# Both weight buffers start 64 bytes further within each partition

## The chip, the cores and the metric

The kernel runs on one core of one Trainium2 chip. The metric is the device time of one execution in microseconds (us); below is the median of three executions. The five engines of the core are called TensorE (PE in the profile, with PEld for its weight loads), VectorE (DVE), ScalarE (ACT), GpSimd (POOL) and SyncE (SP, which issues nearly all the loads here).

## The reference

Two transformer blocks run one after the other on a sequence of 256 tokens of width 1024, all in float32. Cut to what matters:

```
x = x + 0.5 * swiglu(rmsnorm(x), w_gate, w_up, w_down)          # "ff1", d_ff 2816
proj = rmsnorm(x) @ w_in                                        # q, k, v, gMLP and gate inputs
x = x + (g_a * (gmlp(proj) @ w_branch_a) + g_b * (stick(q, k, v) @ w_branch_b)) @ w_out
x = x + 0.5 * swiglu(rmsnorm(x), ...)                           # "ff2"
x = rmsnorm(x)
h = x + moba(rmsnorm(x) @ w_qkv) @ w_o[0]                       # "moba"
h = h + relu(rmsnorm(h) @ w_up[0]) ** 2 @ w_down[0]             # "mlp0", d_ff 4096
h = h + fox(rmsnorm(h) @ w_q, rmsnorm'(h) @ w_kv) @ w_o[1]      # "fox": q and k, v from two norms
h = h + relu(rmsnorm(h) @ w_up[1]) ** 2 @ w_down[1]             # "mlp1"
out = rmsnorm(h)
```

Nearly all the arithmetic is in products of 256 token rows with weight matrices, some 217 MB of weights that are each read once.

## The kernel before

**The weight stream.** Every weight matrix comes in units of at most 128 partitions x 1024 float32. SyncE loads a unit into one of six slots of the tile raw. ScalarE copies it, rounded to the shorter format float32r, into one of eight slots of w_hi (the helper `hi`, line 595). VectorE subtracts, so that w_lo holds the rest (the helper `lo`, line 936). TensorE then takes three products for one: high weights times high activations, high times low and low times high. The semaphores hi_ready, lo_ready and used pass a slot from one to the next, always in the same order of units, which is written out by hand for each engine.

**Which operand is which.** A matmul has a stationary operand, loaded ahead of it into the array by a weight load (LDWEIGHTS, 128 columns), and a moving one, that streams through (256 or 512 columns here). There are three uses of the weights:

- In the first products of the four feed-forward stages (the function `up`), weights are stationary and the transposed activations xt move. Line 1500 takes w_hi times xt_hi and xt_lo together, 512 columns; line 1507 takes w_lo times xt_hi, 256 columns. One chunk has four units, and a unit has eight matmuls of line 1500 and then eight of line 1507 (the fourth unit of a chunk takes them in twos). There are 11 chunks in ff1 and ff2 each and 8 in mlp0 and mlp1 each, 38 in all.
- In the projections of q and k (the function `project`, the shared line 1414), weights are stationary, 128 x 128 at a time, and xt moves with 256 columns, in 24 matmuls a unit. In fox, q is not computed from xt but from xq_hi and xq_lo, and k from xt. A cycle of the attention loop has one unit for q and one for k, 48 matmuls back to back. Three attention stages have 8 such pairs of units each.
- Everywhere else (the functions `rows_times`, `down` and `out_unit`, also line 1414), the activations (xt, yt_hi, yt_lo, ht_hi, ht_lo) are stationary, and weights move, 512 columns.

**Where the tiles lie.** Each tile is a run of bytes in every partition, and tiles lie one behind another in the order of the code, each start rounded up to 32 bytes. Before the change raw, w_hi, w_lo, x, side, xt, yt_hi, yt_lo, ht_hi, ht_lo, the three work tiles, qt, kt, vn and the constants all start at a multiple of 128 bytes, and every slice that a matmul takes of them starts at a multiple of 128 bytes too. Small tiles behind them break this order. So these start 64 bytes past a multiple of 128: xq_hi, xq_lo, dist and nslope, and in the first block a_uv, gates and wst, which share their place. wf_hi and wf_lo (16 columns a slice, line 1414 too) start at a multiple of 128.

Of the kernel before, what the change touches and what calls it, by code (L numbers as in the profile page):

```python
# [25 lines left out]
P = 128  # L26
# [116 lines left out]
def two_blocks(nc, x_in, ff1_norm, ff1_w_gate, ff1_w_up, ff1_w_down, mix_norm, w_in, b_gate, gmlp_ln_g,  # L143
# [4 lines left out]
    with ctx:  # L148
        def sb(name, shape, dt=F32, scope=ctx):
            return scope.enter_context(nc.sbuf_tensor(name, shape, dt))  # L150
# [3 lines left out]


        raw = sb("raw", [P, RAW, WIDE])
        w_hi = sb("w_hi", [P, RING, WIDE], F32R)
        w_lo = sb("w_lo", [P, RING, WIDE], F32R)
        x = sb("x", [P, TOK, D])
        side = sb("side", [P, TOK, D])  # L160
        xt = sb("xt", [P, KT, 2, S], F32R)
# [1757 lines left out]
```

How the kernel before makes its waits and increments, by code:

```python
        def consumed(eng, c, i=0):  # L274
            eng.wait_ge(s["used"], RING + c + 1 + RING * i)
# [4 lines left out]
        @block.sync  # L281
# [1 line left out]
            def room(c, i):  # L283
                sp.wait_ge(s["lo_ready"], RING + c - RAW + 1 + RING * i)
# [80 lines left out]
            def norm_rows():  # L366
                sp.wait_ge(s["sp_done"], HEADS)
                sp.wait_ge(s["r_ready"], HEADS)
                for row, dst in zip((gmlp_ln_g, gmlp_ln_b), ln_rows):
                    sp.dma_start(dst, row.rearrange("a g c -> a (g c)").broadcast_to([P, D])).then_inc(s["blk1_in"], 16)
# [58 lines left out]
            proj_units("w_out", wout, lambda i: 0)  # L430
            ff_units("ff2", ff2_w_gate, ff2_w_up, ff2_w_down)
            att_units("moba", *qkv_moba)
            out_units("w_o0", wo[0])
            mlp_units("mlp0", w_up_2[0], w_down_2[0])
            att_units("fox", *qkv_fox)
            out_units("w_o1", wo[1])
            mlp_units("mlp1", w_up_2[1], w_down_2[1])
            for tok in range(TOK):
                sp.wait_ge(s["second_out"], tok + 1)
                sp.dma_start(out[0, tok * P:(tok + 1) * P, 512:D], side[:, tok, 512:D]).then_inc(s["stored"], 16)
            sp.wait_ge(s["stored"], 32 * TOK)
# [6 lines left out]
            def const(ins, name="const_done"):  # L449
                ins.then_inc(s[name], 1)
                count["n"] += 1
                pool.wait_ge(s[name], count["n"])
# [79 lines left out]
            def pairs(phase):  # L533
                if phase == "fox":
                    pool.wait_ge(s["cn_done"], 1)
                if phase != "stick":
```

## Time and profile before

| | |
|---|---|
| median of 3 executions | 1236.98 us (1236.93 to 1237.11) |
| the profiled execution's own time | 1236.78 us |
| its span, first to last instruction | 1235.0 us |
| TensorE matmul busy | 1222.5 us, 6847 matmuls |
| TensorE weight load busy | 1048.1 us |
| VectorE busy | 835.0 us |
| ScalarE busy | 627.7 us |
| mean DMA rate | 180 GB/s |
| granted TensorE clock | 1.000 of full |

The busy time of TensorE counts each matmul from its start to a modelled end, and these overlap: a matmul of 512 columns is shown with 389 ns while the next one starts some 227 ns after it. So "busy" says that TensorE always has something under way, not that it runs at its peak. What sets the pace within a run of matmuls is the distance from one start to the next.

### The profile page before, as it was taken

Reading aid. Unit: us, or ns where it says so; the run is one execution under the profiler, and the core shown is the slowest. Engines: PE = TensorE matmul, PEld = TensorE weight load, DVE = VectorE, ACT = ScalarE, POOL = GpSimd, SP = SyncE. Lnnn points to the kernel's source line nnn. Section 1 sums busy time; section 2 is a strip of 40 time slices with the busy share of each in tenths; the row PEclk is TensorE's granted clock in tenths of the full one; section 3 lists DMA queues with packets and bytes.
Section 4 is the critical chain, followed back from the end, with each engine's and each line's share of the span. In section 5 each row is a group of like instructions: output and inputs, shape, how many; then the busy total and the mean of one; then the engine's idle time right before and its main releaser. Section 6 shows DMA issues by size and latency. Waiting matters only on the chain.

```text
span 1235.0 us, 17596 instructions
## 1 busy us (share of the span) xinstructions
PE 1222.5 (99%) x6847; PEld 1048.1 (85%) x6847; DVE 835.0 (68%) x1277; ACT 627.7 (51%) x965; POOL 82.9 (7%) x181
## 2 busy tenths in 40 slices
PE   8999999999999999999999999999999999999998
PEld 7888888898888888888888988888888888888886
DVE  6877766454675668777775766875656676876764
ACT  6544446565553446444455656544446455744443
POOL 0000000121000000000003210000000540000000
PEclk9999999999999999999999999999999999999999
DMA  7755666534855555655665445866653655676640
GB/s 237 238 184 186 204 193 194 183 115 115 294 173 169 170 155 175 214 179 186 194 195 169 123 136 188 261 195 191 189 171 105 173 155 166 198 246 189 191 148 35
DMA packets 174923, 221.74 MB, mean 180 GB/s; under 512 B 9100, under 2 KB 103912, under 8 KB 174840
## 3 DMA queue, kind: packets, MB, share of 16 engines
q1 hardware_dynamic: 173496, 216.86, 56.0%
q0 software_dynamic: 912, 2.71, 0.8%
q8 instruction: 54, 0.88, 0.3%
q10 hardware_dynamic: 432, 1.05, 0.2%
q14 instruction: 29, 0.24, 0.1%
HBM read 219.52 MB, written 1.06 MB: 179 GB/s over the span
## 4 chain that ended last, share of the span: by engine, by line
PE 95%; DVE 3%; ACT 1%; DMA 0%; issue 0%; ACTq 0%; DVEq 0%; POOLq 0%
PE bank L1414 55%; PE bank L1500 22%; PE bank L1507 11%; PE bank L1437 1%; PE bank L1671 1%; DVE w_lo L936 1%; PE bank L1654 1%; DVE xt L971 1%; PE bank L1644 1%; PE bank L1631 1%; PE bank L1629 1%; DVE x L1051 0%; PE bank L1675 0%; ACT xt L633 0%; DMA gain_rows<-in_ff_norm 0%; PE bank L1622 0%
## 5 line engine op out<-in xcount | busy, mean ns | idle before, releaser
L936 DVE TENSOR_TENSOR w_lo<-raw,w_hi 128x1024 fp32r<-128x1024 f32 (+1 forms) x448 | 491.4, 1119 | 199.8 <-ACT w_hi L595 199.5
L595 ACT ACTIVATE w_hi<-raw 128x1024 fp32r<-128x1024 f32 (+1 forms) x448 | 422.6, 972 | 277.9 <-PE bank L1507 141.7
L1500 PE MATMUL bank<-xt,w_hi 128*128 128x512 f32 x1216 | 317.0, 393 | 0.0
L1500 PEld LDWEIGHTS bank<-xt,w_hi 128*128 128x128 f32 x1216 | 216.3, 189 | 34.6
L1507 PEld LDWEIGHTS bank<-xt,w_lo 128*128 128x128 f32 x1216 | 170.6, 190 | 15.3
L1507 PE MATMUL bank<-xt,w_lo 128*128 128x256 f32 x1216 | 175.1, 282 | 0.0
L1414 PE MATMUL bank<-w_hi,xt 128*128 128x512 f32 x512 | 159.8, 393 | 0.9 <-DVE xq_lo L971 0.5
L1414 PE MATMUL bank<-w_hi,yt_lo 128*128 128x512 f32 x336 | 132.2, 394 | 0.0
L1414 PE MATMUL bank<-w_hi,yt_hi 128*128 128x512 f32 x336 | 130.9, 390 | 0.0
L1414 PE MATMUL bank<-w_lo,yt_hi 128*128 128x512 f32 x336 | 130.9, 390 | 0.0
L1414 PE MATMUL bank<-xt,w_hi 128*128 128x256 f32 x640 | 116.0, 283 | 0.0
L1414 PEld LDWEIGHTS bank<-w_hi,xt 128*128 128x128 f32 x512 | 94.6, 188 | 23.1 <-issue 3.7
L1414 PE MATMUL bank<-w_lo,xt 128*128 128x512 f32 x256 | 99.8, 390 | 0.0
L1414 PEld LDWEIGHTS bank<-xt,w_hi 128*128 128x128 f32 x640 | 99.5, 191 | 0.2
L989 DVE TENSOR_REDUCE work<-bank 128x256 f32<-128x512 f32 x152 | 96.1, 683 | 0.0
L1414 PE MATMUL bank<-xt,w_lo 128*128 128x256 f32 x320 | 91.8, 287 | 0.0
L1414 PE MATMUL bank<-w_hi,ht_lo 128*128 128x512 f32 x224 | 87.3, 390 | 0.0
L1414 PE MATMUL bank<-w_hi,ht_hi 128*128 128x512 f32 x224 | 87.3, 390 | 0.0
L1414 PE MATMUL bank<-w_lo,ht_hi 128*128 128x512 f32 x224 | 87.2, 389 | 0.0
L1414 PEld LDWEIGHTS bank<-w_hi,yt_lo 128*128 128x128 f32 x336 | 63.1, 188 | 13.9 <-issue 1.0
L1414 PEld LDWEIGHTS bank<-w_lo,yt_hi 128*128 128x128 f32 x336 | 63.1, 188 | 13.3
L1414 PEld LDWEIGHTS bank<-w_hi,yt_hi 128*128 128x128 f32 x336 | 63.1, 188 | 12.9
(197 smaller groups left out, 1149.1 us busy)
## 6 DMA issues: line engine op xcount, KB each, us to landing
raw<-in_w_up SPq DMA_DIRECT2D x64, 512.0 KB, 4.2
raw<-in_w_down SPq DMA_DIRECT2D x64, 512.0 KB, 4.5
raw<-in_w_in SPq DMA_DIRECT2D x56, 512.0 KB, 4.6
raw<-in_ff_w_gate SPq DMA_DIRECT2D x88, 256.0 KB, 3.5
raw<-in_ff_w_up SPq DMA_DIRECT2D x88, 256.0 KB, 4.4
raw<-in_ff_w_down SPq DMA_DIRECT2D x88, 256.0 KB, 4.6
raw<-in_moba_w_qkv SPq DMA_DIRECT2D x24, 512.0 KB, 4.1
raw<-in_w_o SPq DMA_DIRECT2D x16, 512.0 KB, 3.8
```

Of the source, the lines that this page charges most:

```text
L595: act.activation(w_hi[:, c % RING, 0:w], raw[:, c % RAW, 0:w], ACT.Copy).then_inc(s["hi_ready"], 1)
L936: dve.tensor_tensor(w_lo[:, c % RING, 0:w], raw[:, c % RAW, 0:w], w_hi[:, c % RING, 0:w].bitcast(F32), ALU.subtract).then_inc(s["lo_ready" ...
L971: dve.scalar_tensor_tensor(low[:, k, :], src, gain[:, 8 * g + k:8 * g + k + 1], high[:, k, :].bitcast(F32), ALU.mult, ALU.subtract)\
L989: dve.tensor_reduce(work[0][:, q // 2, (q % 2) * S:(q % 2 + 1) * S], up_banks(m)[q][:].rearrange("p (a b) -> p b a", a=2), AX_X, ALU.add)\
L1414: ins = pe.matmul(dst, p, q, start=first and n == 0, stop=last and n == 2)
L1437: ins = pe.transpose(banks[b][:, o:o + P], src[:, tok, k * P:(k + 1) * P], ident[:])
L1500: ins = pe.matmul(up_banks(m)[q][:], w_h[:, k % 2, q * P:(q + 1) * P], flat(xt[:, k, :, :]), start=k == 0, stop=False, skip_group_check=True)
L1507: ins = pe.matmul(up_banks(m)[q][:, 0:S], w_l[:, k % 2, q * P:(q + 1) * P], xt_hi[:, k, :], start=False, stop=k == KT - 1, skip_group_chec ...
L1629: pe.matmul(z[:, 0:P], q[:, 0:P], k[:, 0:P], start=True, stop=True)
L1631: ins = pe.matmul(z[:, P:3 * P], q[:, P:S], k[:, 0:S], start=False, stop=True, skip_group_check=True)
L1644: pe.matmul(z[:, 0:S], ntri[:], sp[:, h, 0:S], start=False, stop=True, skip_group_check=True)
L1654: ins = pe.transpose(t_bank[h][:, o * P:(o + 1) * P], work[1][:, h, o * P:(o + 1) * P], ident[:])
```

## The change

An unused tile of 64 bytes a partition is put between raw and w_hi, and another behind w_lo. w_hi and w_lo start 64 bytes further than before, hence 64 bytes past a multiple of 128. All tiles behind them start 128 bytes further, so their places modulo 128 are what they were. raw stays where it was. No instruction is added, removed or moved, and no order or wait changes.

```diff
         raw = sb("raw", [P, RAW, WIDE])
+        gap_in = sb("gap_in", [P, 16])
         w_hi = sb("w_hi", [P, RING, WIDE], F32R)
         w_lo = sb("w_lo", [P, RING, WIDE], F32R)
+        gap_out = sb("gap_out", [P, 16])
         x = sb("x", [P, TOK, D])
```

For the two operands of a matmul that means: xt, yt and ht lay a multiple of 128 bytes from the weights that they meet, and now lie an odd multiple of 64 bytes from them. xq_hi and xq_lo lay an odd multiple of 64 bytes from them, and now lie a multiple of 128.

## Rows read from the trace of the kernel before

**Rows 1.** The page: span, busy time by engine, chain by engine.
```profile
span 1235.0 us, 17596 instructions
PE 1222.5 (99%) x6847; PEld 1048.1 (85%) x6847; DVE 835.0 (68%) x1277; ACT 627.7 (51%) x965; POOL 82.9 (7%) x181
...
PE 95%; DVE 3%; ACT 1%; DMA 0%; issue 0%; ACTq 0%; DVEq 0%; POOLq 0%
```

**Rows 2.** Waits by engine: who for whom, us in total, times, longest.
```profile
DVE w_lo L936 <- ACT w_hi L595: 199.5, 149, 6.2
ACT w_hi L595 <- PE bank L1507: 141.7, 85, 2.2
...
PE bank L1437 <- DVE x L1051: 1.1, 3, 0.4
...
PE bank L1414 <- DVE xt L971: 0.3, 2, 0.2
```

**Rows 3.** Line 1414 by form: duration min/median/max in ns, first and last start.
```profile
L1414 PE MATMUL bank<-xt,w_hi x640: 274/283/287, 208.6 to 1023.2; 128*128 128x256 f32 x160
...
L1414 PE MATMUL bank<-xt,w_lo x320: 277/283/388, 208.5 to 1022.9; 128*128 128x256 f32 x160
...
L1414 PE MATMUL bank<-w_hi,ht_hi x224: 387/389/395, 35.1 to 1217.6; 128*128 128x512 f32 x112
...
L1414 PE MATMUL bank<-xq_hi,w_hi x64: 276/276/282, 949.8 to 1020.2; 128*128 128x256 f32 x64
L1414 PE MATMUL bank<-xq_lo,w_hi x64: 276/276/281, 949.9 to 1020.3; 128*128 128x256 f32 x64
L1414 PE MATMUL bank<-xt,wf_hi x16: 276/276/279, 947.1 to 949.6; 128*16 128x256 f32 x16
```

**Rows 4.** Lines 1500 and 1507, the same columns.
```profile
L1500 PE MATMUL bank<-xt,w_hi x1216: 387/389/775, 11.0 to 1206.9; 128*128 128x512 f32 x174
...
L1507 PE MATMUL bank<-xt,w_lo x1216: 274/283/285, 13.5 to 1206.5; 128*128 128x256 f32 x174
```

**Rows 5.** Chain in order of time: start us, us, what. The moba loop, then fox.
```profile
688.23 5.96 PE bank L1414 x48
696.50 5.95 PE bank L1414 x48
...
976.95 5.96 PE bank L1414 x48
985.23 5.80 PE bank L1414 x48
...
1017.65 5.80 PE bank L1414 x48
1036.61 11.15 PE bank L1414 x48
1075.08 10.89 PE bank L1414 x48
```

**Rows 6.** Timeline of TensorE in one fox cycle: start us, us, instruction.
```profile
993.61 0.28 PE L1414 MATMUL bank<-xq_lo,w_hi 128*128 128x256 f32 x1
...
995.99 0.28 PE L1414 MATMUL bank<-xq_lo,w_hi 128*128 128x256 f32 x1
...
996.46 0.28 PE L1414 MATMUL bank<-xt,w_lo 128*128 128x256 f32 x1
...
998.61 0.28 PE L1414 MATMUL bank<-xt,w_lo 128*128 128x256 f32 x1
```

**Rows 7.** Timeline of TensorE in one up chunk of ff1.
```profile
59.72 2.00 PE L1500 MATMUL bank<-xt,w_hi 128*128 128x512 f32 x8
61.56 1.12 PE L1507 MATMUL bank<-xt,w_lo 128*128 128x256 f32 x8
62.52 2.00 PE L1500 MATMUL bank<-xt,w_hi 128*128 128x512 f32 x8
```

**Rows 8.** Groups by line and form: count, busy us, mean ns, idle before.
```profile
L633 ACT ACTIVATE xt<-bank,gain 128x256 fp32r<-128x256 f32 x56 | 23.0, 479 | 57.7 <-PE bank L1437 57.7
L633 ACT ACTIVATE xq_hi<-bank,gain 128x256 fp32r<-128x256 f32 x8 | 3.9, 494 | 0.0
L1051 DVE SCALAR_TENSOR_TENSOR x<-bank,rstd_sq,x 128x512 f32<-128x512 f32 x6 | 4.2, 745 | 19.5 <-PE bank L1414 19.5
L1212 DVE SCALAR_TENSOR_TENSOR gates<-bank,rstd,gates 128x512 f32<-128x512 f32 x8 | 5.6, 746 | 6.7 <-PE bank L1414 6.7
```

## The prediction

> **What bounds the kernel.** I read the page first. TensorE has matmuls under way for 1222.5 of 1235.0 us, and the chain that ended last is 95% TensorE [rows 1]. The table of waits says how tight that is: TensorE's own waits on others are single events of under 1.5 us behind the start, while VectorE's splitting of weights stands idle for 199.5 us behind ScalarE, and ScalarE for 141.7 us behind line 1507, that is, behind slots which TensorE has not given back [rows 2]. So the weight stream runs ahead of TensorE and is held back by it. The time is the sum of the distances between TensorE's matmul starts, and nothing else counts unless a change makes another engine late by more than that lead.
>
> The change adds no instruction. It can act only if an access takes another time at another address, so I looked for pairs of rows in which the same instruction meets the same kind of data at another place modulo 128 bytes. The trace has such a pair. Projections of q and k are the same line, the same shape and the same weight slots. In most of them xt moves, a multiple of 128 bytes from the weights; for q in fox xq_hi and xq_lo move, which lie an odd 64 bytes off. The median matmul is shown with 283 ns with xt and with 276 ns with xq against w_hi [rows 3]. The timeline turns this into a distance between starts. From the start at 993.61 to that at 995.99 there are 21 matmuls of q, 113.3 ns each; in the k unit right behind it, from 996.46 to 998.61, there are 18, 119.4 ns each [rows 6]. And the chain shows it in blocks of one q and one k unit, 48 matmuls: the six of moba (two shown) take 5.94 to 5.96 us; of the six in fox five take 5.79 or 5.80 us, and one 5.96 [rows 5]. An odd 64 bytes in one of the two units so saved 0.15 us in five of six blocks.
>
> Three more rows bear on what the cost is. With a stationary operand of 16 columns only (wf_hi), xt moves at 276 ns, though wf_hi lies a multiple of 128 bytes from it [rows 3]: the moving operand alone isn't slow at its place, it is slow beside a full weight load. With 512 columns moving, the usual duration is 389 ns both for activations against w_hi (line 1414) and for line 1500 [rows 3, 4], and the block of 48 of them takes 10.89 us, 226.9 ns each [rows 5]. That is just twice 113.3 ns: these pay nothing extra now. And line 1507, 256 columns, is at 283 ns [rows 4], late like the projections.
>
> **The change part by part.** Of the weight matmuls, those with 256 columns stand to gain, since the distance of their two operands goes from 0 to 64 modulo 128.
>
> Projections: 960 matmuls (640 and 320, [rows 3]) are 40 units of 24. A unit saves 0.15 us (5.95 less 5.80, [rows 5]): 40 x 0.15 = 6.0 us if all do, and 5.0 us at five of six.
>
> q in fox: 8 units lose their odd 64 bytes and fall back to the pace of xt: 8 x 0.15 x 5/6 = 1.0 us lost.
>
> First products of the feed-forward: a unit of eight matmuls of line 1500 and eight of 1507 takes 62.52 - 59.72 = 2.80 us [rows 7]. At the paces without the extra it would be 8 x 0.2269 + 8 x 0.1133 = 2.72 us. Both halves hold some of it: line 1507 takes 0.96 us for 0.91, and line 1500 takes 1.84 us for 1.815, which I read as the first 512-column matmuls behind late ones still being late. The 38 chunks have 152 such units: 152 x 0.08 = 12.2 us at most. But the fourth unit of a chunk mixes its lines in twos, and one block in fox shows that an odd 64 bytes doesn't always settle at the short distance [rows 5]. Nor does any row show weights that are stationary at the odd place. Between 0 and 12.2 us I take two thirds, 8 us, nearer the upper end since the only rows with an odd distance are mostly fast.
>
> All other weight matmuls have 512 columns, 2448 on line 1414 and 1216 on line 1500. No row has such a matmul at an odd distance. From above: a gain is nearly excluded, as they are at twice the fast pace of 256 columns already; their outliers (median 389, most rows' mean 390) are worth 1 or 2 us. From below: they could become late like the 256-column ones, 7 ns each by [rows 3], 3664 x 7 ns = 25.6 us. I take 0, because a weight load's stream lies under the first part of a 512-column matmul just as it lies under the whole of a 256-column one, and there xq shows it harmless.
>
> Splitting: ScalarE writes w_hi, VectorE reads raw and w_hi and writes w_lo, 448 times each. Nearest rows: ScalarE writes xq_hi (odd) in 494 ns and xt in 479; VectorE reads and writes gates (odd) in 746 ns and x in 745 [rows 8]. So between 0 and 15 ns an instruction, 448 x 15 = 6.7 us of ScalarE at most. It is hidden by the 141.7 us and 199.5 us of idling in front of these very instructions [rows 2]; if that cover were gone it would cost those 6.7 us. A TensorE that is faster by 1% takes that much cover and no more. The tiles behind the weights keep their places modulo 128, as do raw and with it all the weight loads, and I count nothing for them.
>
> The sum: 5.0 - 1.0 + 8 = 12 us less. The profiled execution took 1236.78 us around its span of 1235.0, and the median is 1236.98, so both say the same: 1237 - 12 = 1225 us, 1.0% faster. A measurement of this kernel can tell some 0.2%, 2.5 us, from no change.
>
> **The rivals.**
>
> *The place doesn't matter.* What sets xq apart could be that it lies far from the weights, above all other activations, and not the odd 64 bytes; wf_hi lies there too and is also at 276 ns [rows 3]. Then nothing moves, 1237 us. Against it: xt, yt and ht lie over some 40 KB and the weights over 64 KB, and the durations in one form are the same to the nanosecond over all these places. A milder form: only the odd place of the moving operand counts, and the 256-column matmuls, whose moving xt stays even, gain nothing; then some 1 or 2 us come off where weights move, 1235.5 us, again within what can't be told.
> The Trainium skill speaks for this rival. "SBUF — State Buffer", section "Who interferes with whom", gives TensorE two independent read ports, one for the moving operand and one for weight loads, and says that it never waits on anyone; by that the two streams can't disturb each other wherever they lie, and the sum would be 0 us, 1237 us. The trace disagrees at one point already: 283 against 276 ns for one form, with a full and a 16-column weight load [rows 3].
>
> *The 512-column matmuls become slow.* The order in which the two streams meet turns around for them as well. If at the odd distance it is they that pay 7 ns, 3664 of them cost up to 25.6 us, and with the 12 us gained elsewhere the kernel takes 1250 us. It decides the sign from the point where 47% of them (12 of 25.6 us) are slow. For it: slow 512-column matmuls exist (maxima of 395 ns, [rows 3]), and no row shows them at an odd distance. Against it: the same overlap is harmless with 256 columns of xq.
>
> *The full gain.* Every extra of this kind vanishes, in the fourth units of the chunks and in all projections: 12.2 + 6.0 - 1.0 + 1 = 18 us, 1219 us. This bounds the likeliest case.
>
> **How the numbers follow.** The forecast case, a gain of 5 to 18 us with a middle of 12, has 0.62, with a range of its own of 1219 to 1232 us. No effect, or effects that cancel, has 0.20, at 1234.5 to 1239.5. Slow 512-column matmuls have 0.18, from 1239.5 to 1262, mostly in the lower half, since a part of them may be slow. The range for 8 in 10 takes the forecast case but its edge, the case of no effect and the nearest part of the slower one: 1218 to 1240. Faster by over 0.2% has 0.62, within 0.2% 0.20, slower 0.18.
>
> **What would show it.** Right: line 1507 and xt against w_hi and w_lo on line 1414 at a median near 276 ns for 283; xq against w_hi at 283 for 276; the moba blocks of 48 at 5.65 us for 5.95 (both their units gain 0.15), and the fox blocks still near 5.80, with q and k having changed places; a feed-forward unit at 2.72 to 2.76 us for 2.80; the block of 48 with 512 columns still at 10.89 us. Wrong: 512-column medians of 395 ns and blocks of 48 above 11.1 us would be the second rival; all medians as before, the first. If TensorE shows new waits on w_lo, the splitting has lost its cover.

## The result and the profile after

The changed kernel takes 1246.85 us (1246.16 to 1247.25, 6 runs) against 1237.05 us for the kernel before in the same comparison; the ratio is 1.0077, 95% interval 1.0066 to 1.0087. It is 9.8 us slower. The forecast was 1225 us, and the range of 1218 to 1240 us doesn't hold the time. The profiled execution has a span of 1244.4 us, 9.4 more than before.

The page of the changed kernel, its first lines, shows the same picture as [rows 1]. Line numbers are two higher from here on: 1416, 1502 and 1509 are 1414, 1500 and 1507 of before.

```profile
span 1244.4 us, 17596 instructions
...
PE 1232.3 (99%) x6847; PEld 1043.5 (84%) x6847; DVE 835.4 (67%) x1277; ACT 627.6 (50%) x965; POOL 83.7 (7%) x181
...
PE 95%; DVE 3%; ACT 1%; DMA 0%; issue 0%; ACTq 0%; DVEq 0%; POOLq 0%
```

VectorE and ScalarE have the busy time that they had, to 0.4 us. The table of waits has nothing new for TensorE, and the lead of the weight stream is what it was (compare [rows 2]):

```profile
DVE w_lo L938 <- ACT w_hi L597: 203.8, 148, 6.6
...
ACT w_hi L597 <- PE bank L1509: 140.9, 85, 2.1
...
PE bank L1439 <- DVE x L1053: 0.8, 3, 0.3
...
PE bank L1416 <- DVE xt L973: 0.3, 2, 0.2
```

So the same matmuls follow each other at other distances. By form (line 1416 in the first block, 1502 and 1509 in the second; minimum, median and maximum of the duration in ns), against [rows 3] and [rows 4]:

```profile
L1416 PE MATMUL bank<-xt,w_hi x640: 276/279/285, 209.7 to 1030.6; 128*128 128x256 f32 x160
...
L1416 PE MATMUL bank<-w_lo,yt_hi x336: 390/394/401, 52.0 to 1238.3; 128*128 128x512 f32 x168
...
L1416 PE MATMUL bank<-w_hi,ht_hi x224: 392/397/399, 35.1 to 1226.8; 128*128 128x512 f32 x112
...
L1416 PE MATMUL bank<-xq_hi,w_hi x64: 280/283/284, 956.6 to 1027.6; 128*128 128x256 f32 x64
```

```profile
L1502 PE MATMUL bank<-xt,w_hi x1216: 387/392/652, 11.5 to 1215.9; 128*128 128x512 f32 x174
...
L1509 PE MATMUL bank<-xt,w_lo x1216: 275/279/283, 13.6 to 1215.5; 128*128 128x256 f32 x174
```

With 256 columns the forecast has its sign everywhere: xt went from 283 to 279 ns, not to 276, and xq from 276 to 283. The 279 is a middle of two paces: of the 114 runs of eight on line 1509, 73 go at 113.3 ns from start to start and 41 at 117.7 or 117.8, where all but one of the kernel before go at 119.8 or 120.0 (the first distance of a run left out). With 512 columns and weights moving, 389 became 393 to 397. The chain in order of time shows the same in blocks of 48 (moba, fox, then the 512-column products of mlp1), against [rows 5], and the fox blocks rose from 5.80 to 5.90 us:

```profile
693.19 5.85 PE bank L1416 x48
701.36 5.85 PE bank L1416 x48
...
1000.34 5.90 PE bank L1416 x48
1008.55 5.89 PE bank L1416 x48
...
1082.72 11.19 PE bank L1416 x48
```

A block of the 512-column ones takes 11.19 us for 10.89: 0.30 us over 48 matmuls, 6.3 ns each, and there are 2448 of them. That alone is 15.3 us. And in the timeline of ff1 a unit of eight matmuls of each line takes 62.68 - 59.91 = 2.77 us for 2.80 [rows 7]:

```profile
59.91 1.99 PE L1502 MATMUL bank<-xt,w_hi 128*128 128x512 f32 x8
61.73 1.11 PE L1509 MATMUL bank<-xt,w_lo 128*128 128x256 f32 x8
62.68 2.00 PE L1502 MATMUL bank<-xt,w_hi 128*128 128x512 f32 x8
```

For a balance I took every distance from the start of a weight matmul to that of the next matmul in the trace, less the shortest steady one (113.3 ns behind 256 columns, 226.7 behind 512), left out those over 16 ns (waits), and summed by use. These are the "extras" in us, for nine of the kernels; each number is rounded by itself, so a row adds up within 0.2. The first column is the distance in bytes modulo 256 from the stationary to the moving operand: where xt moves / where weights move / where xq moves.

| kernel | distances | weights move, 512 | line 1500, 512 | line 1507, 256 | projections, xt, 256 | xq, 256 | sum | time |
|---|---|---|---|---|---|---|---|---|
| before | 0 / 0 / 192 | 1.6 | 3.7 | 6.3 | 6.0 | 0.4 | 18.0 | 1237.1 |
| changed | 64 / 192 / 0 | 15.7 | 4.3 | 3.0 | 4.2 | 1.2 | 28.2 | 1246.9 |
| all_64 | 0 / 0 / 192 | 1.5 | 3.7 | 6.3 | 6.0 | 0.3 | 17.8 | 1237.3 |
| act_256 | 0 / 0 / 192 | 1.5 | 3.7 | 6.3 | 6.0 | 0.3 | 17.8 | 1237.5 |
| act_64 | 64 / 192 / 64 | 15.7 | 4.2 | 3.0 | 2.8 | 0.6 | 26.3 | 1244.6 |
| w_128 | 128 / 128 / 64 | 13.9 | 7.4 | 6.3 | 5.2 | 0.8 | 33.7 | 1252.1 |
| w_64_far | 192 / 64 / 128 | 6.2 | 7.1 | 1.1 | 1.6 | 1.0 | 17.0 | 1236.2 |
| act_32 | 32 / 224 / 224 | 15.9 | 7.9 | 4.2 | 3.3 | 0.9 | 32.1 | 1250.4 |
| act_96 | 96 / 160 / 32 | 17.8 | 8.0 | 8.2 | 6.2 | 0.6 | 40.8 | 1259.0 |

The extras rose by 10.2 us with the change, the distances left out as waits fell by 0.6, and the span rose by 9.4 and the time by 9.8. So hardly anything else is left to explain. And over the nine kernels the time is the sum of the extras plus some 1219 us, to within 1 us.

### The profile page after: what moved, and what is told of

It reads as the page before. It is cut to its first block, busy times and chain, and to the rows that moved or that the text cites. A ratio compares the mean times of both kernels' runs of the same rounds, so it can differ in the third digit from the quotient of the medians.

```text
span 1244.4 us, 17596 instructions
## 1 busy us (share of the span) xinstructions
PE 1232.3 (99%) x6847; PEld 1043.5 (84%) x6847; DVE 835.4 (67%) x1277; ACT 627.6 (50%) x965; POOL 83.7 (7%) x181
## 4 chain that ended last, share of the span: by engine, by line
PE 95%; DVE 3%; ACT 1%; DMA 0%; issue 0%; ACTq 0%; DVEq 0%; POOLq 0%
PE bank L1416 55%; PE bank L1502 22%; PE bank L1509 11%; PE bank L1439 1%; PE bank L1673 1%; DVE w_lo L938 1%; PE bank L1656 1%; DVE xt L973 1%; PE bank L1646 1%; PE bank L1633 1%; PE bank L1631 1%; DVE x L1053 0%; DMA gain_rows<-in_ff_norm 0%; PE bank L1677 0%; ACT xt L635 0%; PE bank L1624 0%
## 5 line engine op out<-in xcount | busy, mean ns | idle before, releaser
L1502 PEld LDWEIGHTS bank<-xt,w_hi 128*128 128x128 f32 x1216 | 214.7, 188 | 35.4
L1509 PEld LDWEIGHTS bank<-xt,w_lo 128*128 128x128 f32 x1216 | 168.0, 188 | 15.6
L1509 PE MATMUL bank<-xt,w_lo 128*128 128x256 f32 x1216 | 171.6, 278 | 0.0
L1416 PE MATMUL bank<-w_hi,xt 128*128 128x512 f32 x512 | 162.5, 399 | 0.7 <-DVE xq_lo L973 0.4
L1416 PEld LDWEIGHTS bank<-xt,w_hi 128*128 128x128 f32 x640 | 97.8, 188 | 0.2
L1416 PE MATMUL bank<-xt,w_lo 128*128 128x256 f32 x320 | 90.9, 284 | 0.0
L1416 PEld LDWEIGHTS bank<-w_hi,yt_lo 128*128 128x128 f32 x336 | 63.2, 188 | 15.6 <-issue 1.0
```

What stands on the lines that cost most here:

```text
L1416: ins = pe.matmul(dst, p, q, start=first and n == 0, stop=last and n == 2)
L1502: ins = pe.matmul(up_banks(m)[q][:], w_h[:, k % 2, q * P:(q + 1) * P], flat(xt[:, k, :, :]), start=k == 0, stop=False, skip_group_check=True)
L1509: ins = pe.matmul(up_banks(m)[q][:, 0:S], w_l[:, k % 2, q * P:(q + 1) * P], xt_hi[:, k, :], start=False, stop=k == KT - 1, skip_group_chec ...
```

## The experiments

All are the kernel before with other gaps, unless said otherwise. Their ratios are against the kernel before in the same comparison.

**All places moved, no distance changed: all_64.**

```diff
+        gap0 = sb("gap0", [P, 16])
         w_hi = sb("w_hi", [P, RING, WIDE], F32R)
```

> Only the first gap is put in, so the weights and every tile behind them (activations, constants, xq) start 64 bytes further; only raw stays. The distances between the two operands of every matmul are those of before. Theory A (only the distance of the two operands modulo 128 counts): the time of before, 1237 us, with 389 ns for 512-column matmuls, 283 ns for xt and 276 ns for xq with 256. Theory B (the weights' own place modulo 128 counts, odd is late when they move): 1247 us, with about 395 ns for 512 columns on line 1414.

Measured: 1237.29 us, ratio 0.9996 (0.9986 to 1.0007). The weights lie at the odd place here just as in the changed kernel, and nothing is lost. It isn't their place that counts but the distance. The distance from raw to the weights changed here too, and the engines that split the weights work at the odd places, so neither is the cause.

**The activations moved in place of the weights: act_64.**

```diff
+        gap0 = sb("gap0", [P, 16])
         xt = sb("xt", [P, KT, 2, S], F32R)
...
         ht_lo = sb("ht_lo", [P, 4, S], F32R)
+        gap1 = sb("gap1", [P, 16])
```

> The weights stay at a multiple of 128, and xt, yt and ht start 64 bytes further (a gap ahead of xt, another behind ht_lo). Theory A (distance alone): as the changed kernel, 1246 us, with 395 ns on line 1414 with 512 columns; xq keeps its odd distance and so some 276 ns, worth 1 us less. Theory B (the weights' own place): 1237 us, nothing moves. Theory C (the moving operand's own place, odd is late with 512 columns but early with 256, as xq in the kernel before): line 1414 with 512 columns back at 389 ns, line 1507 at 276 ns, line 1500 (xt moves, 512) late at 395 ns, in all 1237 - 8 + 8 = 1237 us.

Measured: 1244.58 us, ratio 1.0059 (1.0044 to 1.0074), with 393 to 397 ns on the 512-column forms of line 1414: theory A. Theories B and C fall. But it is 2.3 us faster than the changed kernel, with the same distances but for xq, and 1 us was expected. The blocks of 48 in moba show where the rest is: they take 5.64 and 5.85 us in turn, at the same distances, where the changed kernel has 5.85 throughout.

```profile
692.79 5.64 PE bank L1416 x48
700.74 5.85 PE bank L1416 x48
```

**The period: w_128, w_64_far, act_256.**

```diff
+        gap0 = sb("gap0", [P, 32])      # w_64_far: 16
         w_hi = sb("w_hi", [P, RING, WIDE], F32R)
         w_lo = sb("w_lo", [P, RING, WIDE], F32R)
+        gap1 = sb("gap1", [P, 32])      # w_64_far: 48; act_256: only this gap, 64
```

> Both gaps are 128 bytes: the weights start 128 bytes further and the activations 256, so their distance changes by 128 bytes and every place modulo 128 stays. If 128 bytes is the period of the effect (theories A to C): the time of before, 1237 us, same medians. If the period is 256 bytes or more: another time, and other medians for 512 columns on line 1414 or for line 1507.

> The first gap is 64 bytes as in the changed kernel and the second 192, so the weights are odd, and the distance from weights to activations is 192 bytes where the changed kernel has 64. If the period is 128: as the changed kernel, 1247 us, 395 ns on line 1414 with 512 columns and 278 ns on line 1507. If the period is 256, so that it matters which of the two operands leads by 64 bytes: another time, with line 1414's 512 columns below 393 ns.

> One gap of 256 bytes behind w_lo: the weights stay, all behind them starts 256 bytes further. Theory D (what counts is the distance from the stationary to the moving operand modulo 256): 1237 us and the medians of before (389 ns for 512 columns, 283 ns for xt and 276 ns for xq with 256). Theory E (the period is 512 bytes or more, or it is the far end of the tiles that counts): another time.

Measured: w_128 1252.14 us (1.0119, 1.0104 to 1.0134), w_64_far 1236.20 us (0.9991, 0.9982 to 1.0001), act_256 1237.45 us (1.0002, 0.9993 to 1.0011). With 128 bytes more between weights and activations the kernel is slower than with 64, though every place modulo 128 is as before. So 128 isn't the period; 256 gives back the time and the medians of before. And it matters which operand leads: w_64_far has the weights where the changed kernel has them, and its opposite distances (192 / 64 for 64 / 192). Its line 1507 and a block each of moba and of the 512-column products:

```profile
L1509 PE MATMUL bank<-xt,w_lo x1216: 276/276/283, 13.9 to 1205.6; 128*128 128x256 f32 x174
```

```profile
688.02 5.66 PE bank L1416 x48
...
1117.93 11.00 PE bank L1416 x48
```

With xt moving at 192, as xq did in the kernel before, a moba block takes 5.66 us, the value that I had forecast for the change (5.65). (Of its six blocks in the first attention stage one takes 5.65 and five take 5.85, at the same distances.) The forecast had taken the 64 of the change for the 192 of xq.

**Smaller steps: act_32, act_96.** One gap behind w_lo, 8 and 24 float32.

> One gap of 32 bytes behind w_lo: the distances from weights to activations are 32 modulo 256 for xt, yt, ht and 224 for xq. If the memory tells places apart in steps of 64 bytes: a time between those of distance 0 (1237 us) and of 64 (about 1245 us) or equal to one of them, line 1507 between 278 and 283 ns. If smaller steps count: a time or medians outside these.

> One gap of 96 bytes behind w_lo: xt, yt, ht at distance 96 modulo 256 from the weights, xq at 32. If the effect goes by the distance in steps of 64 bytes: between the kernels at 64 (about 1245 us) and at 128 (1252 us). If a step that is no multiple of 64 always hurts, as 32 did: 1249 us or more.

Measured: 1250.38 us (1.0108, 1.0091 to 1.0125) and 1259.00 us (1.0176, 1.0161 to 1.0191), the slowest of all. Steps of 32 bytes count. 32 is worse than both its neighbours, 0 and 64, and 96 worse than 64 and 128.

**Which pairs carry the loss and the gain: ytht_64_only, xt_64_only, xt_64.**

```diff
         xt = sb("xt", [P, KT, 2, S], F32R)
+        gap0 = sb("gap0", [P, 16])
         yt_hi = sb("yt_hi", [P, KT, S], F32R)
...
         ht_lo = sb("ht_lo", [P, 4, S], F32R)
+        gap1 = sb("gap1", [P, 48])
```

> The weights and xt stay, yt_hi, yt_lo, ht_hi and ht_lo alone start 64 bytes further, all behind them 256 further. So the moving weights lie 192 modulo 256 ahead of these stationary operands, as in the changed kernel, and every other pair is as before. Theory D (each pair's distance, moving less stationary, modulo 256): the matmuls with yt and ht stationary go to 395 ns and cost 9.8 us, the rest nothing: 1247 us. If another pair had carried the loss: nearer 1237 us.

Measured: 1247.15 us, ratio 1.0081 (1.0066 to 1.0096). The loss of the change is there with nothing moved but yt and ht. The extras of matmuls with yt and ht stationary went from 0.9 to 11.0 us, and those of all other uses changed by 0.4 us at most. Neither raw nor the weights moved, so the splitting has no part in it. Blocks in the chain, projections of moba as before and 512 columns late:

```profile
684.99 5.95 PE bank L1416 x48
...
1128.87 11.20 PE bank L1416 x48
```

xt_64_only has the gap of 16 ahead of xt and 48 ahead of yt_hi; xt_64 has 16 and 16, which leaves yt and ht at 128.

> The weights stay, xt alone starts 64 bytes further, yt, ht and all behind 256 further, so that these and xq keep their distances. Theory D: the projections gain 3.2 us and line 1507 3.3 us, line 1500 loses 0.3 us, the 512-column matmuls with xt stationary lose 4.2 us: 1235 us. With the run that moves yt and ht alone it should add up to the kernel with all activations moved, 1244.6 us, less the xq part.

> The weights stay, xt alone starts 64 bytes further, yt, ht and all else 128: the half of the changed distances that concerns xt, with those of yt and ht left even (0 modulo 256 becomes 128 for yt and ht, 64 for xt). So with yt and ht at 128, by the extras of the kernel with 128: 512-column matmuls with yt and ht stationary cost 8.6 us more than before, those with xt stationary 4.3 us more; line 1507 and the projections gain 6 us: 1237 + 8.6 + 4.3 - 6 = about 1244 us.

Measured: 1238.17 us (1.0005, 0.9996 to 1.0015) and 1245.57 us (1.0068, 1.0053 to 1.0083). They are 3 and 1.6 us above what was expected. In xt_64_only the terms have the expected signs, but the gains are smaller: projections 4.3 us of extras where act_64 had 2.8, line 1507 4.2 where it had 3.0, at the same distance of xt. So a use doesn't have a fixed price at a distance; the surroundings shift it by a microsecond or two.

act_64 and xt_64 show this most plainly. They differ in nothing but the places of yt and ht, 64 bytes; every operand of line 1509 and of the projections has the same address in both. Yet of the 114 runs of eight on line 1509, 70 go at 113.3 ns in act_64 and 39 in xt_64, the others at 117.7, and its extras are 3.0 and 4.1 us. And the fox block that starts near 1000 us takes 5.85 us in act_64, and 5.64 in xt_64:

```profile
1000.04 5.85 PE bank L1416 x48
```

```profile
1000.26 5.64 PE bank L1416 x48
```

yt and ht are no operands of these matmuls. They are operands of other matmuls that ran ahead, and VectorE and ScalarE write them meanwhile; the first is the likelier cause, but no run parts the two.

**Width or role: before_halves, after_halves.** In the function down of the kernel before and of the changed kernel:

```diff
+            def halves(dst, a, b, first, last):
+                for n, (p, q) in enumerate(((a[1], b[0]), (a[0], b[0]), (a[0], b[1]))):
+                    for cols in (slice(0, 256), slice(256, 512)):
+                        ins = pe.matmul(dst[:, cols], p, q[:, cols], start=False, stop=False)
+                return ins
...
-                                ins = three(bank[2 * half + tok][:], part(h_buffers(m), row, tok_cols(tok)),
+                                ins = (three if last or not m else halves)(bank[2 * half + tok][:], part(...),
```

> The kernel before, with each of 1008 matmuls of the function down (chunks after the first and ahead of the last) cut into two of 256 columns with the same stationary operand; the arithmetic is the same. If the width decides which distance is late: at distance 0 the halves go at 120 ns each, 240 for 226.9, and the kernel to 1237 + 13 = 1250 us. If the role decides (moving weights are fine at distance 0 in any width): 113.3 ns each and 1237 us.

> The same cut in the changed kernel, where the moving weights lie 192 modulo 256 ahead of the stationary activations. If the width decides: the halves go at 113.3 to 115 ns as xq did in the kernel before, 227 to 230 for 233.2, and the kernel to 1247 - 6 to 1247 - 3, 1241 to 1244 us, and so below the same cut in the kernel before: the sign of the change turns round in this function. If the role decides: 117 ns or more each and 1248 us or more.

Measured: 1249.96 us (1.0102, 1.0087 to 1.0117) and 1240.13 us (1.0023, 1.0014 to 1.0033). Each half has a weight load of its own (7855 loads in place of 6847). The same 1008 products, cut in two, are 13 us dearer at distance 0 and 7 us cheaper at distance 192; with the cut, the changed places are 9.8 us faster than the old ones. The halves in the kernel before and then in the changed one:

```profile
L1421 PE MATMUL bank<-w_hi,yt_hi x352: 278/283/283, 51.5 to 1207.9; 128*128 128x256 f32 x176
```

```profile
L1423 PE MATMUL bank<-w_hi,yt_hi x352: 276/276/286, 51.9 to 1199.3; 128*128 128x256 f32 x176
```

That is the pair 283 and 276 of xt and xq [rows 3] again, now with weights moving. So it isn't the role that decides at these two distances, but the width. What these runs can't part is the width itself from the number of weight loads for the same columns.

**The weight load under it: before_short, after_short.** Stationary operands of 32 columns for 128 in 1008 matmuls of down; three quarters of their output rows are left out.

```diff
-                                ins = three(bank[2 * half + tok][:], part(h_buffers(m), row, tok_cols(tok)),
+                                cols = P if last or not m else 32
+                                ins = three(bank[2 * half + tok][0:cols, :],
+                                            part(h_buffers(m), row, slice(tok * P, tok * P + cols)),
```

> The same short weight loads (32 of 128 columns, three quarters of the output rows of 1008 matmuls left out) in the kernel before, whose 512-column matmuls are at 389 ns already. Control: 1237 us and blocks of 48 still at 10.89 us, within 1 us; a short load has nothing to take away. If short loads made any matmul faster by themselves: clearly less.

> The changed kernel, but in the function down (chunks after the first and ahead of the last) the stationary activations have 32 columns instead of 128: 1008 matmuls of 512 columns whose weight load is short; three quarters of their output rows are left out. If the moving stream is disturbed by the full weight load under it: these fall from 395 to 389 ns, their blocks of 48 from 11.19 to about 10.9 us, and the kernel to 1247 - 1008 x 6.5 ns = 1240 us. If the odd place of the moving weights is late by itself: 395 ns and 1247 us.

Measured: 1242.60 us (1.0043, 1.0028 to 1.0058) and 1245.90 us (1.0072, 1.0055 to 1.0089). Neither came as expected. With the shorter load the kernel before is 5.4 us slower, and the changed one 1 us faster, which is within what the runs can tell. The blocks of 48 in the chain, one of before_short and one of after_short:

```profile
1123.05 11.12 PE bank L1414 x48
```

```profile
1104.30 11.12 PE bank L1416 x48
```

Both are at 11.12 us, for 10.89 and 11.19 with full loads. With 32 columns these two distances make no difference in such blocks. That the load under a matmul sets the pace is likely but not shown: the edit also leaves a matmul 32 rows of output for 128, and no run changed one without the other. What it does show is that a full load as such isn't the disturbance: at distance 0 the full load is the fastest of the four.

**Only one of the two weight tiles: lo_64.** A gap of 16 between w_hi and w_lo, and 48 behind w_lo.

> Only w_lo starts 64 bytes further; w_hi stays, and all behind starts 256 bytes further. So w_hi keeps its distance and w_lo has 192 modulo 256 to xt. Theory D, from the extras over the short distance between starts that the earlier runs show for each use: line 1507 (w_lo stationary) falls to about 277 ns and gains 5.3 us, line 1500 gains 1 to 2 us behind it, a third of the projections 1.5 us, and a third of line 1414's 512-column matmuls (w_lo moves, 64 from the activations) loses 1.5 us: 1231 us. If it were the sum of all places and not each pair: 1237 us or more.

Measured: 1245.62 us, ratio 1.0069 (1.0054 to 1.0084), 15 us above the expected. Line 1507 has xt at 192 from w_lo here, the very places of w_64_far. Its median is 281 ns, where that kernel has 276:

```profile
L1509 PE MATMUL bank<-xt,w_lo x1216: 276/281/284, 14.2 to 1215.4; 128*128 128x256 f32 x174
```

Its runs of eight in mlp1 go at 117.7 ns from start to start, those of w_64_far at 113.3. What differs is the place of w_hi, and with it the matmuls that run ahead. So one pair of places has more than one steady pace, and act_64 with xt_64 shows that tiles which aren't its operands decide which is taken. That they do so by the matmuls before is my reading.

Line 1507 is the smaller part of the miss. The larger is in the 512-column matmuls of line 1416, whose extras are 12.6 us where the kernel before has 1.6 and some 3 were expected. Two thirds of them have w_hi moving, at distance 0 as before the change, and these went from 0.9 to 8.3 us; one form of them is 395 ns for the 389 of [rows 3]:

```profile
L1416 PE MATMUL bank<-w_hi,ht_hi x224: 387/395/398, 35.7 to 1226.6; 128*128 128x512 f32 x112
```

Only the third matmul of each three, with w_lo moving, has a new distance. So matmuls whose own distance has stayed at the best value become late when w_hi and w_lo no longer lie alike: the rule by distances was seen to hold only where the two weight tiles moved together. Two paces side by side stand in the kernel before already, in the one late and the five early fox blocks [rows 5].

**The best places found: xt_192.**

```diff
+        gap0 = sb("gap0", [P, 48])
         xt = sb("xt", [P, KT, 2, S], F32R)
...
+        gap1 = sb("gap1", [P, 16])
         yt_hi = sb("yt_hi", [P, KT, S], F32R)
```

> xt alone starts 192 bytes further, and yt, ht and all behind 256; the weights stay. Theory D, with the extras that the earlier runs show for each use: the projections gain 4.4 us and line 1507 5.3 us, line 1500 loses 3.5 us, the 512-column matmuls with xt stationary lose 1.2 us, those with yt and ht keep their 389 ns: 1232 us. If the places of the weights alone counted: 1237 us.

Measured: 1231.22 us, ratio 0.9954 (0.9939 to 0.9969), 5.9 us faster than the kernel before and 15.6 faster than the changed one. One block of moba and one of the 512-column products:

```profile
685.73 5.64 PE bank L1416 x48
...
1113.61 10.90 PE bank L1416 x48
```

256-column products with xt moving have their short distance, and the 512-column ones with yt and ht stationary keep theirs. Line 1500 pays for it with 7.1 us of extras for 3.7.

## Why the prediction was wrong

**What bounds the kernel** was right: the time is the sum of the distances between TensorE's starts. That the change works by the distance between the two operands, and not by the weights' own place, was right too (all_64 against act_64), and so the rival in which the place doesn't matter fell.

**Where it failed** is the term for "all other weight matmuls", taken as 0 because "there xq shows it harmless". It measured +14.1 us (1.6 to 15.7 us of extras in the 2448 of line 1414; the 1216 of line 1500, which had 3.7 us already, changed by 0.6 us in all). Two things were wrong in this one step. It carried a distance that is good with 256 columns over to 512; before_halves and after_halves show the order of the two distances turned round by cutting 512 columns into 256. Nothing in the trace of before had spoken for that step: the same rows show 256 columns late and 512 columns on time at distance 0, and that alone said that width changes the answer. And it sorted distances modulo 128, with an "odd" and an "even"; the period is 256 (w_128 against act_256), and 64 and 192 are different cases (w_64_far).

**First products and projections** had their sign and were mis-sized by the same sorting. Line 1507 with line 1500 gained 2.8 us (10.0 to 7.2 us of extras) for a forecast of 8, the projections 1.9 us for 5.0. The forecast gave each of them one pace, and line 1509 has two in the changed kernel. The row of xq that priced them is at 192, the changed kernel puts xt at 64. At 192 (xt_192) the two are worth 1.6 us (the loss of line 1500 taken in) and 5.2 us.

**A row read wrongly.** The prediction says that wf_hi lies a multiple of 128 bytes from xt. That is so for its start, but its slices are 64 bytes long, so that every second of them lies an odd 64 off. All 16 matmuls take 276 to 279 ns, so the reading that a short load leaves the 256-column matmuls fast stands; with 512 columns before_short doesn't bear it out.

**q in fox** lost 0.8 us for a forecast of 1.0. **The splitting** cost nothing: the same busy times, no new wait, the same lead.

The sum by the forecast's own terms: +14.1 for 0, -2.8 for -8, -1.9 for -5.0, +0.8 for +1.0, together +10.2 for -12. The rival of slow 512-column matmuls, held at 0.18, is what happened, in its milder part: its price of 7 ns was 6.3, its place line 1414 without line 1500. Its time of 1250 us assumed all 3664 late and 12 us gained elsewhere.

**The rule weighed there**, from the Trainium skill, "SBUF — State Buffer", section "Who interferes with whom", is that TensorE's two read ports are independent and that it never waits on anyone. The runs contradict what I drew from it, that the two streams can't disturb each other wherever they lie: places alone move this kernel from 1231.2 to 1259.0 us, at the same instructions.

**What stays open** is the mechanism. The runs show that, with w_hi and w_lo moved together, the price depends on the distance modulo 256 from stationary to moving operand, in steps of 32 bytes or less, and on the width, and that more than these enters: the places of tiles that only other matmuls take (act_64 with xt_64), and w_hi and w_lo lying alike or not (lo_64). They don't show how a load's reads and a matmul's meet, nor which load counts for a matmul, its own or the next one's. Adding up prices by pairs of operands came within 1 us of the measured time in before_halves, after_halves (lower end), ytht_64_only and xt_192, missed by 1.6 and 3 us in xt_64 and xt_64_only, and by 15 us in lo_64.

## What to carry to other kernels

Where TensorE streams back to back, check the distance from one start to the next against the best that the same form reaches anywhere in the trace; here up to 41 us of 1259 lay in differences of a few ns a matmul that no table of waits shows. A row for one width, one sign of the distance or one neighbourhood doesn't price another: a placement has to be tried, one tile at a time, with distances taken modulo 256 or more, and tiles that take turns as operands, as w_hi and w_lo do, kept alike. And if a matmul's cost turns out to depend on where its operands lie, an edit that merely adds a small tile ahead of others can move a time by 1%, so fix the places before two versions are compared.

## What the runs showed of the hardware

- Float32r matmuls of 256 columns behind each other have a steady distance of 113.3 ns at best, and 117.7 or 120 ns at other distances of their operands, at some of them in turn with 113.3; those of 512 columns 226.7 ns at best, and 233 ns on average in the changed kernel, mostly 231 and 236. The granted clock was 1.0 in both kernels, to 0.002.
- 256 bytes more between weights and activations change nothing (1237.5 us for 1237.1); 96 bytes cost 21.9 us (1259.0 us).
- Stationary operands of 32 columns in 512-column matmuls were no better than those of 128: blocks of 48 took 11.12 us for 10.89 at distance 0.
- At one pair of places line 1507 had a median of 276 ns in one kernel (w_64_far) and 281 ns in another (lo_64). In act_64 the moba blocks took 5.64 and 5.85 us in turn, at the same distances.
- With only w_lo moved by 64 bytes, 512-column matmuls with w_hi moving at an unchanged distance lost 7.3 us in all.
